# The first weight chunk of a two-block transformer kernel, fetched as four transfers of one k-tile each

## The reference, cut to what matters

```python
mod_l = (jax.nn.silu(c) @ w_ada[l] + b_ada[l])[:, None, :]
mod_c = (jax.nn.silu(c_ctx) @ w_ada[l] + b_ada[l])[None, None, :]
sh_a, sc_a, gt_a, sh_f, sc_f, gt_f = jnp.split(mod_l, 6, axis=-1)
h_l = modulate(rms_norm(x, g_mix_norm[l]), sh_a, sc_a)
h_c = modulate(rms_norm(xc, g_mix_norm[l]), csh_a, csc_a)
qa_l, kva_l, kr_l, cb_l, cc_l, ch_l = split_projection(h_l @ w_in[l])
```

## Time and profile before

| | us |
|---|---|
| median of 3 runs | 2293.16 |
| lowest and highest | 2291.65, 2293.56 |
| the profiled execution | 2295.6 |
| its span, first to last instruction | 2293.9 |
| TensorE busy | 2254.8 |
| VectorE busy | 1594.5 |
| ScalarE busy | 1093.2 |

### The profile page before, as it was taken

The page is one execution under the profiler, slowest core; times in us unless marked ns, Lnnn a source line. Parts: engine busy times, 40 slices in busy tenths (PEclk is TensorE's granted clock), DMA queues, the critical chain, the costliest instruction groups (busy, mean ns, idle before and its releaser), DMA issues.

```text
span 2293.9 us, 35206 instructions
## 1 busy us (share of the span) xinstructions
PE 2254.8 (98%) x15336; PEld 2039.7 (89%) x15336; DVE 1594.5 (70%) x1877; ACT 1093.2 (48%) x1109; POOL 41.9 (2%) x80
## 2 busy tenths in 40 slices
PE   8999999999999999999999999999999999999998
PEld 3679878999988888888888899999999999999998
DVE  3977997998888556665667778765576644536684
ACT  4665444335455345543454534445345436664353
POOL 0000000000000000000000000000000000000000
PEclk9999999999999999999999999999999999999999
DMA  9775876795776555555555454434545553335543
GB/s 377 295 275 221 307 284 234 284 364 199 293 262 234 197 185 186 194 189 185 191 193 193 158 182 157 146 121 152 183 163 188 183 192 136 128 130 183 184 166 129
DMA packets 64938, 471.59 MB, mean 206 GB/s; under 512 B 7216, under 2 KB 7216, under 8 KB 8336
## 3 DMA queue, kind: packets, MB, share of 16 engines
q1 hardware_dynamic: 55152, 399.21, 47.6%
q0 software_dynamic: 9488, 68.03, 7.9%
q10 hardware_dynamic: 144, 2.10, 0.2%
HBM read 467.21 MB, written 2.10 MB: 205 GB/s over the span
## 4 chain that ended last, share of the span: by engine, by line
PE 83%; DVE 11%; ACT 3%; issue 2%; DMA 1%; DVEq 0%; SPq 0%; ACTq 0%
PE acc L2051 54%; PE aux L2051 29%; DVE lo L1051 4%; DVE ada_acc L1071 2%; ACT hi L426 2%; DMA ada_raw<-ada_stream 0%; DVE rstd L1192 0%; ACT probs L835 0%; DVE columns L1820 0%; DVE probs L1816 0%; DVE rope_scratch L1733 0%; ACT y L519 0%; DMA raw<-stream 0%; DVE u L1734 0%; DVE columns L1345 0%
## 5 line engine op out<-in xcount | busy, mean ns | idle before, releaser
L1051 DVE TENSOR_TENSOR lo<-raw,hi 128x2048 fp32r<-128x2048 f32 x366 | 835.7, 2288 | 482.4 <-ACT hi L426 481.8
L426 ACT ACTIVATE hi<-raw 128x2048 fp32r<-128x2048 f32 x366 | 698.5, 1911 | 721.0 <-PE acc L2051 544.5
L2051 PE MATMUL acc<-act_both,hi 128*128 128x256 f32 (+1 forms) x6208 | 882.7, 299 | 8.8 <-ACT act_both L702 3.9
L2051 PEld LDWEIGHTS acc<-act_both,hi 128*128 128x128 f32 x6208 | 814.7, 193 | 49.6 <-issue 16.5
L2051 PE MATMUL acc<-act_both,lo 128*128 128x256 f32 x3472 | 455.7, 284 | 0.3
L2051 PEld LDWEIGHTS acc<-act_both,lo 128*128 128x128 f32 x3472 | 437.9, 193 | 4.3 <-DVE lo L1051 0.7
L2051 PE MATMUL aux<-act_both,hi 128*128 128x512 f32 (+1 forms) x1152 | 242.6, 361 | 0.0
L2051 PEld LDWEIGHTS aux<-act_both,hi 128*128 128x128 f32 x1152 | 193.7, 189 | 29.6
L1071 DVE SCALAR_TENSOR_TENSOR ada_acc<-ada_raw,silu_c,ada_acc 128x512 f32<-128x512 f32 x224 | 152.9, 745 | 3.5 <-DMA ada_raw<-ada_stream 3.0
L2051 PEld LDWEIGHTS aux<-act_both,lo 128*128 128x128 f32 x992 | 127.4, 191 | 4.3
L2051 PE MATMUL aux<-act_both,lo 128*128 128x256 f32 x992 | 130.9, 283 | 0.0
(11 more groups left out here) (349 smaller groups left out, 1827.5 us busy)
## 6 DMA issues: line engine op xcount, KB each, us to landing
raw<-stream SPq DMA_DIRECT2D x374, 1024.0 KB, 4.8
ada_raw<-ada_stream POOLq DMA_DIRECT2D x64, 1024.0 KB, 5.2
x<-x_t SPq DMA_DIRECT2D x1, 2048.0 KB, 16.0
ctx<-ctx_t SPq DMA_DIRECT2D x1, 2048.0 KB, 13.6
x<-x_t ACTq DMA_DIRECT2D x1, 2048.0 KB, 8.3
out<-x SPq DMA_DIRECT2D x3, 512.0 KB, 7.4
p_raw<-p_t POOLq DMA_DIRECT2D x1, 512.0 KB, 3.8
out<-x SPq DMA_DIRECT2D x2, 256.0 KB, 2.0
```

Source lines behind the costliest of these rows:

```text
L426: nc.scalar.activation(HI[c % NH][:, :], RAW[c % NR][:, :], ACT.Copy).then_inc(hi_done, 1)
L1051: V.tensor_tensor(LO[c % NR][:, :], RAW[c % NR][:, :], HI[c % NH][:, :].bitcast(F32), ALU.subtract)\
L2051: return TE.matmul(out, lhs, rhs, start=start, stop=stop, skip_group_check=True)
```

## The change

SyncE fetches chunk 0 as four transfers of 128 x 512, one k-tile each. The first three raise semaphores of their own, the fourth raises `raw_full[0]`, so that the count of that buffer for later chunks stays as it was. TensorE waits for each of the four ahead of the matmul on its k-tile, in place of one wait for the chunk.

The other edits make room for three more semaphores. The names "nf" and "n2" join the norms that share semaphores for their totals, and the semaphores of squares and high parts get other names; `a_hi`, `ffn_hi`, `late_squares` and `n2_squares` stand where `n2_hi`, `nf_hi`, `nf_sq` and `n2_sq` stood. No instruction is added or moved by that.

```diff
@@ -307,7 +307,7 @@
-    NORMS = {"nx": (2, 0, 4), "nc": (2, 0, 4), "nkv": (1, 1, 1), "nq": (1, 1, 1)}
+    NORMS = {"nx": (2, 0, 4), "nc": (2, 0, 4), "nkv": (1, 1, 1), "nq": (1, 1, 1), "nf": (0, 0, 0), "n2": (0, 0, 0)}
@@ -369,6 +369,12 @@
                 if c == 6:
                     eng.dma_start(CTX[:, :, :], ctx_t).then_inc(sem("ctx_loaded"), 16)
+                if c == 0:
+                    for k in range(4):
+                        part = slice(512 * k, 512 * k + 512)
+                        eng.dma_start(RAW[0][:, part], stream[0][:, part])\
+                            .then_inc(sem(f"first_part{k}") if k < 3 else raw_full[0], 16)
+                    continue
                 eng.dma_start(RAW[c % NR][:, :], stream[c]).then_inc(raw_full[c % NR], 16)
...
@@ -2244,8 +2250,11 @@
                 if n < WHOLE:
-                    pe.wait_ge(raw_full[c % NR], 16 * (c // NR + 1))
+                    if c:
+                        pe.wait_ge(raw_full[c % NR], 16 * (c // NR + 1))
                     for k in range(4):
+                        if c == 0:
+                            pe.wait_ge(sem(f"first_part{k}") if k < 3 else raw_full[0], 16)
                         ins = mm(AUX[0:2, 2 + n % 2, :], whole_c[:, 4 * j + k, :], RAW[c % NR][:, 512 * k:512 * k + 512],
                                  j == 0 and k == 0, j == 3 and k == 3)
                     ins.then_inc(pe_chunk, 1)
@@ -2466,11 +2475,11 @@
-                pe.wait_ge(sem("nf_sq"), k - 10)
+                pe.wait_ge(sem("late_squares"), k - 10)
                 ins = mm(AUX[:, 0, 0:T], ONES[:, :], Y[:, k, :], False, k == 15)
-            ins.then_inc(sem("nf_tot"), 1)
+            ins.then_inc(step("nf_tot")[0], 1)
```

More of the change, by code:

```diff
@@ L692, in _ @@
                     act.wait_ge(acc_free, PH["w_out"][1] + 3)
-                    nc.scalar.activation(Y[:, 0:12, :], X[:, 0:12, :], ACT.Square).then_inc(sem("nf_sq"), 1)
+                    nc.scalar.activation(Y[:, 0:12, :], X[:, 0:12, :], ACT.Square).then_inc(sem("late_squares"), 1)
             for t in range(4):
@@ L697, in _ @@
                 s = slice(12 + t, 13 + t)
-                nc.scalar.activation(Y[:, s, :], X[:, s, :], ACT.Square).then_inc(sem("nf_sq"), 1)
+                nc.scalar.activation(Y[:, s, :], X[:, s, :], ACT.Square).then_inc(sem("late_squares"), 1)
             root("nf", T)
@@ L702, in _ @@
                 nc.scalar.activation(AH[:, k, :], Y[:, k, :], ACT.Identity, bias=MOD[:, 3 * KD + k:3 * KD + k + 1])\
-                    .then_inc(sem("nf_hi"), 1)
+                    .then_inc(sem("ffn_hi"), 1)
                 if k == 7:
@@ L773, in _ @@
             act.wait_ge(acc_free, last)
-            nc.scalar.activation(Y[:, 0:12, :], X[:, 0:12, :], ACT.Square).then_inc(sem("n2_sq"), 1)
+            nc.scalar.activation(Y[:, 0:12, :], X[:, 0:12, :], ACT.Square).then_inc(sem("n2_squares"), 1)
             split(c0)
@@ L779, in _ @@
                 s = slice(12 + t, 13 + t)
-                nc.scalar.activation(Y[:, s, :], X[:, s, :], ACT.Square).then_inc(sem("n2_sq"), 1)
+                nc.scalar.activation(Y[:, s, :], X[:, s, :], ACT.Square).then_inc(sem("n2_squares"), 1)
             root("n2", T)
@@ L786, in n2_high @@
                         act.wait_ge(sem("n2_scaled"), k + 1)
-                        nc.scalar.activation(AH[:, k, :], X[:, k, :], ACT.Copy).then_inc(sem("n2_hi"), 1)
+                        nc.scalar.activation(AH[:, k, :], X[:, k, :], ACT.Copy).then_inc(sem("a_hi"), 1)
                     return
@@ L790, in n2_high @@
                 nc.scalar.activation(AH[:, 4 * q:4 * q + 4, :], X[:, 4 * q:4 * q + 4, :], ACT.Copy)\
-                    .then_inc(sem("n2_hi"), 1)
+                    .then_inc(sem("a_hi"), 1)
             n2_high(0)
@@ L1526, in _ @@
                 if m == 44:
-                    dve.wait_ge(sem("nf_sq"), 1)
+                    dve.wait_ge(sem("late_squares"), 1)
                     twelve_to_three("nf_ss")
@@ L1539, in low_of @@
                 for k in range(4 * q, 4 * q + 4):
-                    dve.wait_ge(sem("nf_hi"), k + 1)
+                    dve.wait_ge(sem("ffn_hi"), k + 1)
                     V.scalar_tensor_tensor(out=AL[:, k, :], in0=Y[:, k, :], scalar=MOD[:, 3 * KD + k:3 * KD + k + 1],
@@ L1656, in _ @@
             last = PH["down2"][1] + 3
-            dve.wait_ge(sem("n2_sq"), 1)
+            dve.wait_ge(sem("n2_squares"), 1)
             twelve_to_three("n2_ss")
@@ L1682, in n2_low @@
             def n2_low(q):
-                dve.wait_ge(sem("n2_hi"), q + 4)
+                dve.wait_ge(sem("a_hi"), q + 4)
                 s = slice(4 * q, 4 * q + 4)
@@ L2468, in _ @@
             for k in range(12, 16):
-                pe.wait_ge(sem("nf_sq"), k - 10)
+                pe.wait_ge(sem("late_squares"), k - 10)
                 ins = mm(AUX[:, 0, 0:T], ONES[:, :], Y[:, k, :], False, k == 15)
-            ins.then_inc(sem("nf_tot"), 1)
+            ins.then_inc(step("nf_tot")[0], 1)
             def nf_ready(j):
-                return (sem("nf_hi"), 4 * j + 4), (sem("ffn_ready"), 4 * j + 4)
+                return (sem("ffn_hi"), 4 * j + 4), (sem("ffn_ready"), 4 * j + 4)
             for n, (a, b) in enumerate(PARTS):
@@ L2507, in _ @@
             for k in range(12, 16):
-                pe.wait_ge(sem("n2_sq"), k - 10)
+                pe.wait_ge(sem("n2_squares"), k - 10)
                 ins = mm(AUX[:, 0, 0:T], ONES[:, :], Y[:, k, :], False, k == 15)
-            ins.then_inc(sem("n2_tot"), 1)
+            ins.then_inc(step("n2_tot")[0], 1)
             pe.wait_ge(sem("consts2_loaded"), 16)
@@ L2513, in _ @@
             c0, g0 = PH["iq"]
-            group(c0, g0, AH, AL, ready=lambda j: ((sem("n2_hi"), j + 4), (sem("a_ready"), j + 1)), low_last=True, by_k=1)
+            group(c0, g0, AH, AL, ready=lambda j: ((sem("a_hi"), j + 4), (sem("a_ready"), j + 1)), low_last=True, by_k=1)
             side_by_side(c0 + 4, g0 + 1, A2, spare=True)
```

## The result

The changed kernel takes 2297.23 us (median of 11 runs; before: 2293.56 of 11), a ratio of 1.0017 with an interval of 1.0009 to 1.0024: some 3.7 us slower, where the forecast was 2293.3 and its range ended at 2296.5. The prediction stood on the 2293.16 of before's first three runs, so 0.4 us of the distance to it is that choice; the change itself was forecast at +0.15 us and measured at +3.7. Beside other kernels on another chip it was 2297.84 against 2293.60, ratio 1.0016 (1.0007 to 1.0025).

What follows compares the result with a forecast made beforehand. TensorE and DMA were both taken as full early on, with chunk 4's landing deciding. Start -2.1, new wait +2.04 and smaller packets +0.2 made +0.15 us on 2293.16, so 2293.3 us; range 2290.2 to 2296.5.

Steps and rivals of the forecast that it cites:

- The gain of the start: At chunk 0, TensorE begins once the first piece lands, 2.1 us earlier: -2.1 us.
- one pause: In front of chunk 4, TensorE newly waits 1 to 2 us for its transfer: +2.04 us in the sum.
- one line: On the DMA engines, transfers are served in order of issue, one chunk (1.05 MB) every 2.5 us.
- to the end one for one: From chunk 4 on TensorE has no pause until 47.26 us, so the +0.15 us passes to the end.
- The renames: Renamed and shared semaphores add no instruction and no wait: 0 us.
- I had 4.9: At chunk 0's first piece, TensorE's first pass was expected near 4.9 us, 2.1 us earlier.
- Smaller packets: +0.2: Chunk 0's 2 KB rows take about 85 ns per packet, delaying everything that lands later by 0.2 us.
- DMA can't run dry: While the pieces are issued, one per 0.49 us is 540 GB/s against 426 moved, so the backlog holds.
- the bound of +2.4: Upper limit of the packet term, if the pieces' packets went at 212 GB/s like the vectors' slice: +2.4 us.
- The slack: At chunk 4, TensorE's idle of 0.40 us against the usual 0.34 left 0.06 us to spare.
- The rival that came true in part: TensorE's clock falls in the new pause at chunk 4: 1.7 us, giving 2295.0 us; chance 12%.
- The rival that is refuted: Each extra transfer costs up to 2.2 us on the DMA engines, 6.6 us for three: 2299.8 us; chance 4%.

Runs made afterwards that it cites:

- e4: Kernel before with chunk 0 whole, plus one extra 0.67 MB transfer queued between the constants and chunk 4: 2294.64 us (+1.0, ratio 1.0003).
- e10: Kernel before with two extra transfers (1.72 MB) ahead of chunk 4 and four unused matmuls behind chunk 3: 2297.13 us (+3.6, ratio 1.0016).
- e2: Kernel before with only the renamed and shared semaphores, chunk 0 fetched whole with one wait: 2293.99 us (+0.4, ratio 0.9999).
- e1: The changed kernel, unaltered, run once more beside others on one chip, against the kernel before: 2297.84 us (+4.2).
- e9: Kernel before with two extra transfers (1.72 MB) ahead of chunk 4, chunk 0 unsplit, nothing filling the pause: 2299.98 us (+6.4, ratio 1.0024).
- e7: The change with each piece of chunk 0 stored as one block of memory, four transfers and four waits: 2294.41 us (+0.6 on before, ratio 1.0003).
- e6: Kernel before with chunk 0 as one transfer of 512 rows of 2 KB, stored k-tile by k-tile, one wait: 2294.70 us (+0.9, ratio 1.0006).
- e11: Against the kernel before, chunk 0 as two transfers of two k-tiles each, rows of 4 KB, two waits: 2295.30 us (+1.8, ratio 1.0008).

## Why the prediction was wrong

**Right.** The gain of the start is lost in front of chunk 4, in one pause ended by its transfer. All transfers are one line, and TensorE's lateness at chunk 4 goes to the end one for one (e4: 1.0 and +1.0; e10: 3.3 and +3.6; the table of the rest of the span). The renames cost nothing (e2). TensorE started at 5.6 us, where I had 4.9.

**The term that was mis-sized.** "Smaller packets: +0.2" took one duration for all packets (85 ns, or 83 if the line through the two rows is drawn at its 38 ns per KB; measured 84 at the median but 108 to 125 in the mean) and forgot the time in which none was there. The sentence before it, that one piece per 0.49 us of issue is 540 GB/s and DMA can't run dry, took SyncE's issue for the supply of the engines. The share of 0.55 from 4 to 5 us shows it did run dry. The term measured 1.6 us on chunk 4's landing in the first trace and 2.2 to 2.5 in the others, where I had 0.2: about the bound of +2.4 that I had written down and then hardly used for the range.

**The slack.** I read 0.06 us from the weight loads. But TensorE loads a pass's weights while the pass before runs, so chunk 4's first pass started later than 22.76: its eight passes take 3.52 us up to the columns, so it was at 26.65 - 3.52 = 23.1, and the slack was 0.4 us. This error went the other way.

**The rival that came true in part.** The fall of the clock had 12% and 1.7 us. The price was right (1.5 and 1.7 us in e1 and e9). Its chance was put for a pause of 2.1 us; with the lateness it was 2.9. It adds to the lateness instead of standing in its place: 1.8 to 2.2 us of the 3.6 measured are lateness by the transfer, and the rest, some 1.4 us, is clock as far as the rough reckoning goes. Only a part of it can be the fall at chunk 4, which one trace in four has. My range let the cases stand one by one, so the sum of two (0.15 + 1.6 + 1.7 and the scatter of runs) lay beyond its end.

**The rival that is refuted.** A cost of 1.5 us or more for each transfer would have shown in e7, which has four of them and a chunk 4 that lands 0.5 us and starts 0.15 us late; e6, with one, moved no more bytes. The Trainium skill ("DMA: Bandwidth & Descriptors", section "Rules for kernel authors") wants large transfers; that came out on the right side here, for a cause that these two runs do not bear out. The Trainium skill's page "TensorE: Matmul & The Clock Gate", section "HAM oscillation — how this bites in real kernels", was the better warning, with its clock lost in waits for transfers. This happened in one of the change's four traces, in front of chunk 4, and not between the pieces. Filling the pause with matmuls nobody needs made two kernels faster by 2.2 and 2.9 us in the medians, 1.4 and 1.8 in the means.

Open is how often the fall at chunk 4 comes (one in four traces, though the mean clock of the runs says 1.4 us), why the falls later on differ from trace to trace, and so whether the pause has a hand in them.

## What to carry to other kernels

Before you split a first transfer so that the consumer can start early, look for the transfer at which the consumer catches up with the line again; if the line is full until then, as here, the split could only cost. Here a piece cut out of longer rows of memory moved more slowly than the whole; stored one behind the other, the pieces lost half as much of the line. And when two rivals can hold at once, the range has to reach to their sum.

## What the hardware showed that was not expected

- Rows of 2 KB cut out of 8 KB rows: 131 to 340 GB/s at the start, against 405 for whole rows. The same rows stored contiguously: 0.97 MB in place of 0.66 from 3 to 6 us. Rows of 4 KB (e11): 0.94 MB there, but chunk 4's semaphore takes 1.9 us from its first to its last step, in place of 1.0.
- Four transfers into 32 partitions each instead of one into 128: 0.88 MB in place of 1.65 from 4 to 8 us, with the engines full in both.
- SyncE's issue of a transfer took 0.43 us as long as few were queued and 0.67 to 1.50 us for the eighth in the change's four traces.
- An idle of 2.0 to 4.1 us on TensorE comes with a granted clock of 0.50 in some executions and not in others of the same kernel: in the change 2.86 us with, 2.90, 2.87 and 2.87 without; with contiguous pieces 2.02 us with, 2.88 without.
